# Sums and maxima of a sequence taken four pages at a time, weight splits moved last, and signals and copies rearranged in a fused attention and gMLP decoder step

## The reference

```python
h = rmsnorm(x); proj = h @ w_in            # 1024 -> 5632: q k v g_a u v_s g_b m_a m_b
attn = moba(q, k, v)                       # block-sparse attention, T5 relative bias
y_a = attn * silu(g_a)
y_b = gelu(u) * spatial_mix(layernorm(gelu(v_s))) * silu(g_b)
mixed = sigmoid(m_a) * (y_a @ w_pa) + sigmoid(m_b) * (y_b @ w_pb)
y = rmsnorm(x + mixed @ w_o)
```

## Time and profile before

| | |
|---|---|
| median of three runs | 599.32 us (597.98 to 601.37) |
| the profiled execution | 598.01 us, of which the span 595.9 us |
| TensorE busy | 574.4 us, 96%, granted clock 0.997 |
| VectorE, ScalarE busy | 312.3 us (52%), 213.0 us (36%) |
| DMA | 111.9 MB, mean 188 GB/s |
| one tanh of 544 columns (L945) | 650 ns |
| one copy of the turned probabilities (PT) | 594 ns |

### The profile page before, as it was taken

How to read it: one execution, slowest core, us unless ns; L and a number is a source line. 1 busy time by engine, 2 the same in 40 slices (tenths; PEclk the granted TensorE clock), 3 DMA queues, 4 the chain that set the end, 5 groups by cost and what they waited for, 6 DMA issues and landing times.

```text
span 595.9 us, 15270 instructions
## 1 busy us (share of the span) xinstructions
PE 574.4 (96%) x6260; PEld 538.7 (90%) x6260; DVE 312.3 (52%) x693; ACT 213.0 (36%) x467; POOL 27.5 (5%) x39
## 2 busy tenths in 40 slices
PE   7999999999999999999999989999999989999993
PEld 5999999998889899899889978998989989999992
DVE  5633324336448446656856654884362373692316
ACT  5422223325334433444544341332342231242242
POOL 2101112000000000000000000120000000000002
PEclk9999999999999999999999999999999999999998
DMA  8447424665685675766758568785789566323003
GB/s 265 123 161 231 126 95 150 206 184 172 199 246 173 215 232 171 251 189 211 223 161 265 178 216 261 242 257 174 247 281 307 191 203 223 113 74 122 21 1 150
DMA packets 74888, 111.91 MB, mean 188 GB/s; under 512 B 5418, under 2 KB 39219, under 8 KB 74820
## 3 DMA queue, kind: packets, MB, share of 16 engines
q1 hardware_dynamic: 73588, 107.59, 57.1%
q0 software_dynamic: 1232, 3.36, 2.0%
HBM read 106.39 MB, written 4.53 MB: 186 GB/s over the span
## 4 chain that ended last, share of the span: by engine, by line
PE 81%; DVE 11%; ACT 3%; issue 2%; DMA 1%; SPq 0%; POOL 0%; DVEq 0%; ACTq 0%; POOLq 0%
PE BK L475 45%; PE BK L620 8%; PE BK L495 7%; PE BK L632 4%; PE BK L646 4%; PE BK L556 2%; PE BK L696 2%; DVE WL L1061 1%; PE BK L713 1%; PE BK L703 1%; DMA SGC<-in_gating_constants 1%; ACT SC L952 1%; DVE NMX L1253 1%; ACT APX L965 1%; PE BK L672 1%
## 5 line engine op out<-in xcount | busy, mean ns | idle before, releaser
L475 PE MATMUL BK<-XH,WH 128*128 128x272 f32 x672 | 212.7, 316 | 0.0
L475 PE MATMUL BK<-XH,WL 128*128 128x272 f32 x672 | 194.2, 289 | 0.0
L475 PE MATMUL BK<-XL,WH 128*128 128x272 f32 x672 | 193.2, 288 | 0.0
L475 PEld LDWEIGHTS BK<-XH,WH 128*128 128x128 f32 x672 | 126.6, 188 | 9.9 <-issue 8.7
L475 PEld LDWEIGHTS BK<-XL,WH 128*128 128x128 f32 x672 | 127.2, 189 | 0.0
L475 PEld LDWEIGHTS BK<-XH,WL 128*128 128x128 f32 x672 | 126.5, 188 | 0.0
L1061 DVE TENSOR_TENSOR WL<-WRAW,WH 128x1024 fp32r<-128x1024 f32 x59 | 72.2, 1223 | 87.6 <-ACT WH L847 87.4
L620 PE MATMUL BK<-CST,KRAW 128*128 128x128 f32 x512 | 77.1, 273 | 2.4 <-DVE ATS L1238 2.2
L1158 DVE COPY KT<-BK 128x512 f32<-128x512 f32 x64 | 44.2, 690 | 57.1 <-PE BK L620 56.7
L847 ACT ACTIVATE WH<-WRAW 128x1024 fp32r<-128x1024 f32 x60 | 63.2, 1054 | 21.3 <-PE BK L495 21.3
L620 PEld LDWEIGHTS BK<-CST,KRAW 128*128 128x128 f32 x512 | 60.2, 140 | 4.5 <-issue 4.1
(11 more groups left out here) (196 smaller groups left out, 804.4 us busy)
## 6 DMA issues: line engine op xcount, KB each, us to landing
KRAW<-in_cache_k SPq DMA_DIRECT2D x128, 256.0 KB, 3.3
VRAW<-in_cache_v SPq DMA_DIRECT2D x120, 256.0 KB, 3.8
WRAW<-in_w_in SPq DMA_DIRECT2D x21, 1024.0 KB, 5.7
WRAW<-in_w_o SPq DMA_DIRECT2D x4, 1024.0 KB, 5.2
XR<-in_x_prompt SPq DMA_DIRECT2D x4, 512.0 KB, 6.3
VEX<-in_cache_v SPq DMA_DIRECT2D x8, 256.0 KB, 4.3
WRAW<-in_w_pb SPq DMA_DIRECT2D x4, 512.0 KB, 6.5
WRAW<-in_w_pa SPq DMA_DIRECT2D x4, 512.0 KB, 4.9
```

The source lines that it names most:

```text
L475: last = mm(BK[h][:, 0:HALF], w[:, n % 2, k, :], x[:, k, cols], start=(i == 0 and w is WH and x is XA), stop=(i == KC - 1 and w is WL))
```

## The change

- **Sums.** `block_sums` becomes `page_sums(q)`, called in every fourth step: it takes sum and maximum of the 128-column part of SCB that has just been scored; for a sequence's last part it also adds the bias, and `gate_rows` makes R. It stands ahead of the weight split.
- **Splits.** `split_lo` is the last of the frame's VectorE work in a step with t % 4 == 0, behind the sums, `local_out` (moved from step 5 to step 4 of 16) and the prompt copy.
- **Gate sums** go to the head of the step on TensorE, ahead of the page transposes.
- **Exponentials** each add to `ex_ok`, so 5 for a sequence; each transpose of probabilities waits for its own.
- **Output and gating.** `sample_out` goes from step 6 to step 5 of 16, `prompt_gate` ahead of `silu`; the gelu instructions shift by one step. XH and XL are made in four pieces in steps 133 to 136. On SP the gMLP constants are issued in step 83 instead of 84, the gating constants first.

```diff
# SP
-                if t == 84:
+                if t == 83:
                     sp.wait_ge(av_ev, 16)
+                    sp.dma_start(SGC[:], sgc).then_inc(sgw_ld, 16)
                     sp.dma_start(WSR[:], w_s[0].rearrange("g t s -> t g s")).then_inc(sgw_ld, 16)
-                    sp.dma_start(SGC[:], sgc).then_inc(sgw_ld, 16)
# TensorE
             def turn_probs(b, t):
-                pe.wait_ge(ex_ok, b + 1)
                 for x in range(4):
+                    pe.wait_ge(ex_ok, 5 * b + x + 1)
                     last = pe.transpose(bk[:, x * P:(x + 1) * P], SC[:, x * P:(x + 1) * P], IDN)
             for t in range(STEPS):
+                if t % 16 == 1 and t > 16 and t < 144:
+                    gate_sums(t // 16 - 1, t)
                 if t < PAGES:
                     turn_page(t)
# ScalarE
-                if t % 4 == 2 and 54 <= t < 86:
-                    gelu_tanh((t - 54) // 4)
                 if t % 16 == 2 and t > 16 and t < 144:
                     exponentials(t // 16 - 1)
                 if t % 4 == 3 and 19 <= t < 83:
                     prompt_exp(t // 4 - 4)
+                if t % 4 == 3 and 55 <= t < 87:
+                    gelu_tanh((t - 55) // 4)
-                if t == 130:
+                if 133 <= t < 133 + PAIRS:
+                    c = t - 133
                     act.wait_ge(av_ev, 16)
                     act.wait_ge(pj, matmuls_before(T_PB))
-                    copy(XH[:, 0:4, 0:SEQ], G[:, GA:GA + 4, 0:SEQ]).then_inc(yah_ok, 1)
+                    copy(XH[:, c, 0:SEQ], G[:, GA + c, 0:SEQ]).then_inc(yah_ok, 1)
# VectorE
+            def page_sums(q):
+                b, x = q // 4, q % 4
+                dve.wait_ge(sc_pe, q + 1)
+                if x == 0:
+                    wait(dve, r_ok, b)
+                sc = SCB[:, x * P:(x + 1) * P]
+                summed = dve.tensor_reduce(KP[:, 0, x:x + 1], sc, AX.X, ALU.add)
+                if x == 3:
+                    link(summed)
+                    last_page = SCB[96:128, 3 * P:4 * P]
+                    link(dve.tensor_tensor(last_page, last_page, B15, ALU.add))
+                peak = dve.tensor_reduce(KP[:, 1, x:x + 1], sc, AX.X, ALU.max)
+                if x == 3:
+                    link(peak)
+                    gate_rows(b)
...
+                if t % 4 == 0 and 4 <= t <= PAGES:
+                    page_sums(t // 4 - 1)
+                if t % 16 == 4 and t >= 20 and t < 144:
+                    local_out(t // 16 - 1)
+                if t % 4 == 0 and 20 <= t < 84:
+                    prompt_out(t // 4 - 5)
+                if t % 4 == 0 and 4 <= t <= 128:
                     split_lo(n + 1)
+                if t % 4 == 2 and 22 <= t < 86:
+                    prompt_gate(t // 4 - 5)
...
-                if t % 4 == 2 and 22 <= t < 86:
-                    prompt_gate(t // 4 - 5)
-                if t % 16 == 6 and t >= 38:
+                if t % 16 == 5 and t >= 37:
                     sample_out(t // 16 - 2)
-                if t % 16 == 0 and t >= 16 and t < 144:
-                    block_sums(t // 16 - 1)
```

More of the change, by code:

```diff
@@ L628, in page_scores @@
                 if x == 0:
-                    wait(pe, ex_ok, b)
+                    wait(pe, ex_ok, 5 * b)
                 for c in range(PAIRS):
@@ L676, in turn_local @@
                 bk = other_bank(t)
+                pe.wait_ge(ex_ok, 5 * b + 5)
                 pe.transpose(bk[0:32, 64:96], SCL[:], IDN[0:32, 0:32])
@@ L768, in filling @@
                     if u < 2:
-                        pe.wait_ge(yal_ok, u + 1)
+                        pe.wait_ge(yal_ok, PAIRS + u)
                     yield from branch(n, x, h, 16 + u, XH, XL)
@@ L784, in _ @@
                             page_values(v)
-                if t % 16 == 1 and t > 16 and t < 144:
-                    gate_sums(t // 16 - 1, t)
                 if t % 16 == 3 and t > 16 and t < 144:
@@ L952, in exponentials @@
                     act.activation(SC[:, x * P:(x + 1) * P], SCB[:, x * P:(x + 1) * P], ACT.Exp, bias=EB[:, x:x + 1], scale=1.0 / UNIT,
-                                   accum_out=L2[:, x:x + 1])
+                                   accum_out=L2[:, x:x + 1]).then_inc(ex_ok, 1)
                 act.activation(SCL[:], LOCS[:, b, :], ACT.Exp, bias=NEGM[0:32, :], scale=1.0 / UNIT, accum_out=L2[0:32, 4:5]).then_inc(ex_ok, 1)
@@ L1185, in gate_product, with gate_rows @@
                 dve.tensor_tensor(G[:, GB + c], G[:, GB + c], G[:, GU + c], ALU.mult).then_inc(ug_ok, 1)
[L1187 to L1193, removed]
+            def page_sums(q):
[13 more added lines that the diff above has]
+                    gate_rows(b)
+            def gate_rows(b):
                 own, pair, kp = CST[:, C_OWN:C_OWN + 4], CST[:, C_PAIR:C_PAIR + 2], KP[:]
@@ L1377, in _ @@
                 if t == 142:
-                    dve.wait_ge(yah_ok, 2)
+                    dve.wait_ge(yah_ok, PAIRS + 1)
                     dve.tensor_tensor(XL[:, 0:4, SEQ:ROWS], G[:, GA:GA + 4, SEQ:ROWS], f32(XH[:, 0:4, SEQ:ROWS]), ALU.subtract).then_inc(yal_ok, 1)
@@ L1381, in _ @@
                     scale_out(t // 16 - 2)
-                if t % 16 == 5 and t >= 20 and t < 144:
-                    local_out(t // 16 - 1)
                 if t % 2 == 1 and t < PAGES:
                     page_out(t)
-                if t % 4 == 2 and 22 <= t < 86:
-                    prompt_gate(t // 4 - 5)
-                if t % 16 == 6 and t >= 38:
-                    sample_out(t // 16 - 2)
-                if t % 16 == 0 and t >= 16 and t < 144:
-                    block_sums(t // 16 - 1)
                 if t % 16 == 1 and t >= 16 and t < 144:
                     choose(t // 16 - 1)
+                if t % 16 == 5 and t >= 37:
+                    sample_out(t // 16 - 2)
                 if t % 4 == 2 and 18 <= t < 82:
@@ L1397, in _ @@
                     prompt_norm(t // 4 - 4)
-                if t % 4 == 0 and 20 <= t < 84:
-                    prompt_out(t // 4 - 5)
-                if t % 4 == 1 and 53 <= t < 85:
-                    gelu_inner((t - 53) // 4)
-                if t % 4 == 3 and 55 <= t < 87:
-                    gelu_outer((t - 55) // 4)
+                if t % 4 == 2 and 54 <= t < 86:
+                    gelu_inner((t - 54) // 4)
+                if t % 4 == 0 and 56 <= t < 88:
+                    gelu_outer((t - 56) // 4)
                 if t % 4 == 1 and 85 <= t < 101:
@@ L1418, in _ @@
                     dve.tensor_tensor(YBL[:], G[:, GB:GB + 4, :], f32(YBH[:]), ALU.subtract).then_inc(ybl_ok, 1)
-                if t == 130:
-                    dve.wait_ge(yah_ok, 1)
-                    dve.tensor_tensor(XL[:, 0:4, 0:SEQ], G[:, GA:GA + 4, 0:SEQ], f32(XH[:, 0:4, 0:SEQ]), ALU.subtract).then_inc(yal_ok, 1)
+                if 133 <= t < 133 + PAIRS:
+                    c = t - 133
+                    dve.wait_ge(yah_ok, c + 1)
+                    dve.tensor_tensor(XL[:, c, 0:SEQ], G[:, GA + c, 0:SEQ], f32(XH[:, c, 0:SEQ]), ALU.subtract).then_inc(yal_ok, 1)
                 if t >= 129:
```

## The result

| | kernel before | changed kernel |
|---|---|---|
| median | 598.65 us (597.94 to 601.37, 4 runs) | 591.12 us (590.25 to 592.63, 4 runs) |
| ratio | | 0.987, 95% interval 0.983 to 0.990 |
| the profiled execution (span) | 598.01 us (595.9) | 590.25 us (588.2) |

The forecast was 592.5 us and a sum of 6.2 us (taken from the median of 599.3 that stood there, the sum gives 593.1); the medians differ by 7.5 us, the two profiled executions by 7.76. Timed again beside the last experiment, the changed kernel took 591.91 us (590.20 to 592.74, 6 runs) against 599.65 (597.71 to 600.33, 11 runs), ratio 0.987 (0.985 to 0.990).

What follows compares the result with a forecast made beforehand. TensorE, busy 96% of the span, bounds the kernel, so only its waits count. 0.54 + 1.07 + 0.9 + 3.45 + 0.3 - 0.06 = 6.2 us: 591.8, or 593.1 from the median; stated 592.5, 8-in-10 range 589.8 to 596.8.

Steps and rivals of the forecast that it cites:

- constants (L720): TensorE's wait at the mixing weights for the gating constants goes whole when they are loaded earlier: 0.54 us.
- output copy, step 102: Page transposes at 404.25 no longer wait for the copy of the turned output: 0.91 plus 0.16, 1.07 us.
- output copy, step 86: Page transposes at 356.14 start near 355.25 through the earlier output copy: 0.9 of 1.5 us won, bounds 0.4 and 1.48.
- sequence 4: Probability transposes: single signals 0.61 plus tanh behind exponentials 0.65, cap 1.10; tanh then delays a copy, 0.84 us left.
- sequence 5: Probability transposes: the wait of 0.21 goes whole, up to its cap of 0.37 us.
- sequence 6: Probability transposes: single signals 0.61 plus a choice 0.13 earlier, 0.74 us, under a cap of 0.81.
- sequence 7: Probability transposes: single signals 0.61 plus a choice 0.95 earlier, under a cap of 1.52 + 0.16; taken as 1.5 us.
- sequence 3: Prompt scores' wait of 0.90 shrinks by 0.44 through earlier gating, though the choice is 0.45 later; 0.3 us lasts.
- sequence 0: Gate sums: R comes 1.1 us sooner but is asked for 1.2 sooner; the 0.40 wait stays, counted as -0.06 us.
- Only the late part wins: Rival: choice later than counted in sequences 1 to 4, losing 0.3 and 0.84; 594.4 us (595.9 not claimed; median terms 595.7), chance 0.15.
- Handed back: Rival: TensorE reaches K pages and weights 6 us earlier and waits there; 597 to 599 us, 0.12 together with waits moving on.
- The slower rival: VectorE's queue bounds the gate sums; up to 1.2 us new wait in each of 8 sequences; 601 or 602.5 us, chance 0.07.

Runs made afterwards that it cites:

- the last experiment, E9: Changed kernel with the weight split ahead of the sums in step 64 alone and the last outer gelu product moved to step 85; 591.73 us.
- E1: Kernel before with only the gMLP constants issued in step 83 instead of 84, gating constants first; 598.94 us, timed once.
- E6: Changed kernel with the weight split ahead of the page sums again; 591.53 us, timed once.
- E8: Changed kernel with three outer gelu products moved behind the choice, gating or output copy, and sequence 0's gate sums back in mid-step; 590.18 us.
- E2: Kernel before with only the copy of the turned output moved from step 6 to step 5 of 16; 598.61 us, ratio 0.998.
- E3: Kernel before with only single signals: each exponential signals and each transpose of probabilities waits for its own; 596.23 us, ratio 0.995.
- E7: Changed kernel with XH and XL made in one piece in step 130 again; 593.5 us, timed once.
- E4: Changed kernel with all eight gate sums back in the middle of the step; 591.81 us, ratio 0.988.
- E5: Changed kernel with sums and maxima of all four pages at once (512 wide) in the new place; 592.72 us, timed once.

## Why the prediction was right, and where its sizes were off

The time fell in the forecast range because the waits named were the ones that went, one after the other, and next to nothing took the gain back. The sum of 6.2 us was 1.6 us short of the lead of 7.8, by small parts of many terms. That the 592.5 us lay only 1.4 above the median of 591.12 is in part luck: by the sum it would have been 593.1, and no reason was given for going lower. The leads between places give each term its measured size (changed kernel):

| term | forecast | measured |
|---|---|---|
| constants (L720) | 0.54 | 0.75 |
| output copy, step 102 | 1.07 | 1.10 |
| output copy, step 86 | 0.90 | 0.87 |
| sequence 4 | 0.84 | 0.95 |
| sequence 5 | 0.37 | 0.44 |
| sequence 6 | 0.74 | 0.78 |
| sequence 7 | 1.50 | 1.87 |
| sequence 3 | 0.30 | 0.45 |
| sequences 1 and 2 | 0 | 0.25 |
| sequence 0 | -0.06 | 0.21 |
| step 71 to 82 | 0 | 0.11 |
| sum | 6.2 | 7.8 |

- **Constants.** The term was mis-sized by a rule that the prediction itself gave: a start is 0.16 us later than the idle time says. 0.54 + 0.16 = 0.70; E1 shows 0.76. I had added the 0.16 everywhere else.
- **Output copy.** Right at both steps, down to what is left: step 86 still waits, 0.46 us. E6, E8 and E9 confirm what it waits for: with the split or the product out of the copy's way it goes, and 0.62 to 0.64 us with it. What I did not see is that this gain depends on the constants (E2). In the changed kernel they were early, so it did not matter.
- **Single signals and choice, sequences 4 to 7.** E3 gave 0.66 for one sequence by the signals alone, the forecast 0.61. Sequence 6 stayed under its cap, sequence 5 came 0.07 over it. In sequence 4, 0.3 us more came than by the signals; the prediction puts that down to the tanh moved behind the exponentials, which no run moved by itself. In sequence 7 several parts of the change act together: without XH's move the gain is 0.85 less (E7: 6.89 - 5.87 = 1.02), without the gate sums at the head 0.59 less (E4), with wide sums 0.81 less (E5). I capped it at the wait of 1.52 + 0.16 and overlooked that TensorE also stood at the gate sums of this sequence, the second of the two waits for R in the earlier trace rows:

```profile
478.70 0.37 PE L666 MATMUL BK<-R,CST 128*128 128x24 f32 x2 [0.19 <-DVE R L1197]
```

It is gone in the changed kernel, and is worth 0.19 + 0.16. With it the waits come to 2.04; the values behind, which started 0.09 us after the modelled end of the matmul ahead (at 485.94) and now start 0.07 before such an end (at 478.21), give 0.16; the transposes take 1.05 instead of 0.63 us and take 0.42 back. That makes 1.78 of the 1.87.

- **Sequence 3.** The walk along VectorE was right (choice 0.46 later, gating sooner), the wait at the prompt scores 0.59 as against the "near 0.5" that I had given. No run moved the gelu product or the gating by itself, so their share rests on this walk. The tanh that I feared would take back 0.14 did so in sequence 4 only (0.19 for PT), so 0.45 came instead of 0.30.
- **Sequences 0 to 2.** In sequence 0, R waits 0.1 longer, as forecast. But there, too, TensorE's transposes of the probabilities had stood 0.18 us, less than a row of the timeline shows, and E3 gives 0.21 for ending it. Sequences 1 and 2 lost waits of 0.12 us at the prompt scores. I had looked only at waits that the list names.
- **The rivals.** "Only the late part wins" fell: sequence 4 won 0.95 and sequence 3 0.45. "Handed back" fell: no wait for a page or weight appeared, DMA went from 0.77 to 0.79. The slower rival fell by the reserve at R, 1.4 us in sequence 3; with the wide sums (E5) its mechanism is real, a wait of 1.3 us in sequence 0, but in that sequence alone at this size. By the Trainium skill's VectorE: DVE Perf Modes, section on the TRN2 errata, tiles of 512 or more are to be preferred; the page gives this for sources in SBUF, and the reductions here read PSUM, so it was no full rival. What E5 measures for this place is the reverse, 2.5 us in favour of the small ones. That agrees with the Trainium skill's Perfetto Trace Analysis, Optimizing Scalar/DVE Operations, by which breaking up instructions may help where VectorE is not saturated (54% busy here) and holds up another engine.
- **The expected signs.** All came: no wait at the mixing weights, none at step 102, none at L672, 64 reductions near 0.29, the gate sums' wait 0.5 in one sequence only. The waits of the lines concerned were 3.3 + 2.2 + 0.9 + 0.6 + 0.5 = 7.5 us and are 0.6 + 0.5 + 0.5 + 0.2 = 1.8, so 5.7 less where I had said about 5.5. The lead is 2.1 larger than that. Most of it is the 0.16 us and more that each of the seven listed waits which went hides, 1.1 us at the least, and the unlisted waits of sequences 0 to 2 and of step 81, 0.6.

## What to carry to other kernels

Where one engine is busy 96% of the time, list its waits, find for each the instruction of the other engine that stood in front, and move that one: here nine short waits of 0.2 to 1.5 us, seven ended and two shortened, made up most of the gain, while the helping engine got more to do. Before believing a gain, ask what stands next on the same queue (E3: XH; E8: an activation that waits for the product moved) and whether a transfer with a date of its own comes after it (E2). And where the scatter of the times is as large as the effect, count from one instruction to another within the trace.

## What the runs showed of the hardware

- The first 12 us have two lengths. The four 512-column matmuls of L516 take 634 to 672 ns each in one kind of execution (5 of 12) and 1092 to 1096 in the other, while the granted clock reads 1.00 for the microseconds from 1 to 12 in both. The first page transpose comes 1.7 to 2.4 us later than in the kernel before in the second kind. What decides is not in the profile and was not tried.
- With that taken off, the two executions of the changed kernel agree within 0.03 us at all page transposes over 430 us. This holds where TensorE waits for no transfer. The gating constants, issued behind the mixing weights, took 5.8 us to land in the kernel before, 5.3 in E2 and 5.5 in E3, and TensorE waited 0.54 us, 1.27 us and not noticeably; a lead counted across such a wait holds the scatter of the transfer too.
- An idle time in the timeline understates a late start by 0.16 us or somewhat more: E1 removed one listed with 0.54 and led by 0.76, the changed kernel one of 0.91 (step 102) and won 1.10, one of 0.21 (sequence 5) and won 0.44. Short waits do not show at all: E3 ended one in sequence 0 worth 0.21 that no list names.
